# Two constant tiles multiplied by TensorE in the waits of three LayerNorms

## What is computed

```python
def _layer_norm(x):
    xc = x - jnp.mean(x, axis=-1, keepdims=True)
    return xc * lax.rsqrt(jnp.mean(xc * xc, axis=-1, keepdims=True) + LN_EPS)
...
        u = _layer_norm(h) * (1.0 + sc1) + sh1
        z = u @ w_in[l]
        ...
        mix = (gate_a * y_a + gate_b * y_b) @ w_out[l]
        h = _layer_norm(DEEPNORM_ALPHA * h + g1 * mix) * ln1_w[l] + ln1_b[l]
        u2 = _layer_norm(h) * (1.0 + sc2) + sh2
        a, bb = jnp.split(u2 @ w_ffn_in[l], 2, axis=-1)
        ffn = (jax.nn.silu(a) * bb) @ w_ffn_out[l]
        h = _layer_norm(DEEPNORM_ALPHA * h + g2 * ffn) * ln2_w[l] + ln2_b[l]
```

## Time and profile before

| | us |
|---|---|
| median of three runs | 3309.01 (3307.96 to 3311.09) |
| the profiled execution | 3308.02 |
| its span | 3305.9 |
| TensorE busy in it | 3128.1 (95%) |
| ScalarE, VectorE, GpSimd busy | 1085.3, 1153.4, 1440.2 |

### The profile page before, as it was taken

How to read it: one execution, slowest core, us unless ns; L and a number is a source line. 1 busy time by engine, 2 the same in 40 slices (tenths; PEclk the granted TensorE clock), 3 DMA queues, 4 the chain that set the end, 5 groups by cost and what they waited for, 6 DMA issues and landing times.

```text
span 3305.9 us, 52329 instructions
## 1 busy us (share of the span) xinstructions
PE 3128.1 (95%) x20668; PEld 2496.1 (76%) x20668; DVE 1153.4 (35%) x1637; ACT 1085.3 (33%) x1516; POOL 1440.2 (44%) x1824
## 2 busy tenths in 40 slices
PE   6998989988999899999988999999999999899999
PEld 4887768857887586887666888788688866688877
DVE  5016442332111355322555422225632255442210
ACT  2445453323222324112444322222411244432222
POOL 3542234634555363322415655566322241555555
PEclk7999889989999899999999999999999999999999
DMA  4223332212333232222414232233221241423233
GB/s 192 95 89 118 112 119 85 95 55 70 101 95 98 72 117 73 88 66 102 152 55 156 91 97 95 96 108 122 73 87 63 100 159 55 153 89 101 95 96 121
DMA packets 101407, 330.85 MB, mean 100 GB/s; under 512 B 9856, under 2 KB 10112, under 8 KB 100224
## 3 DMA queue, kind: packets, MB, share of 16 engines
q1 hardware_dynamic: 74656, 273.85, 25.3%
q10 hardware_dynamic: 26592, 54.66, 4.5%
HBM read 299.64 MB, written 28.84 MB: 99 GB/s over the span
## 4 chain that ended last, share of the span: by engine, by line
issue 41%; POOL 30%; PE 24%; DMA 1%; DVE 1%; ACT 1%; DVEq 0%; POOLq 0%; SPq 0%; ACTq 0%
POOL w_lo L310 30%; PE psum L339 19%; PE psum L620 4%; DMA w_raw<-in_fills 1%; DMA H<-scratch 1%; DVEq L1409 0%; PE psum L796 0%; POOLq L306 0%; PE psum L816 0%; PE psum L834 0%; POOLq L316 0%; DVE HL L1412 0%; PE psum L836 0%; DVE arena L1966 0%; PE psum L830 0%
## 5 line engine op out<-in xcount | busy, mean ns | idle before, releaser
L310 POOL TENSOR_TENSOR w_lo<-w_raw,w_hi 128x256 fp32r<-128x256 f32 x1820 | 1440.0, 822 | 1860.8 <-ACT w_hi L870 1664.9
L339 PE MATMUL psum<-XH,w_hi 128*128 128x512 f32 x2592 | 1061.8, 410 | 35.7 <-DVE XL L1412 22.5
L339 PE MATMUL psum<-XH,w_lo 128*128 128x512 f32 x2592 | 1021.2, 394 | 0.0
L339 PE MATMUL psum<-XL,w_hi 128*128 128x512 f32 x2592 | 1019.8, 393 | 0.0
L870 ACT ACTIVATE w_hi<-w_raw 128x1024 fp32r<-128x1024 f32 x436 | 460.2, 1056 | 813.6 <-PE psum L339 717.7
L339 PEld LDWEIGHTS psum<-XH,w_hi 128*128 128x128 f32 x2592 | 493.5, 190 | 174.0 <-issue 59.2
L339 PEld LDWEIGHTS psum<-XL,w_hi 128*128 128x128 f32 x2592 | 492.6, 190 | 106.3
L339 PEld LDWEIGHTS psum<-XH,w_lo 128*128 128x128 f32 x2592 | 493.7, 190 | 103.7 <-issue 9.4
L339 PE MATMUL psum<-HH,w_hi 128*128 128x512 f32 x976 | 391.6, 401 | 29.5 <-DVE HL L1412 21.5
L339 PE MATMUL psum<-HL,w_hi 128*128 128x512 f32 x976 | 387.0, 397 | 0.0
L339 PE MATMUL psum<-HH,w_lo 128*128 128x512 f32 x976 | 386.7, 396 | 0.0
(11 more groups left out here) (302 smaller groups left out, 2385.6 us busy)
## 6 DMA issues: line engine op xcount, KB each, us to landing
w_raw<-in_fills SPq DMA_DIRECT2D x488, 512.0 KB, 3.6
scratch<-arena ACTq DMA_DIRECT2D x86, 256.0 KB, 2.0
arena<-scratch ACTq DMA_DIRECT2D x10, 1024.0 KB, 8.7
arena<-in_w_ada SPq DMA_DIRECT2D x4, 2048.0 KB, 20.1
H<-scratch ACTq DMA_DIRECT2D x4, 2048.0 KB, 15.7
scratch<-H SPq DMA_DIRECT2D x2, 2048.0 KB, 8.5
arena<-scratch ACTq DMA_DIRECT2D x2, 2048.0 KB, 9.9
arena<-scratch ACTq DMA_DIRECT2D x2, 1792.0 KB, 20.8
```

The costliest lines, as they stand in the source:

```text
L310: ins = nc.gpsimd.tensor_tensor(w_lo[:, to:to + FILL // 4], w_raw[:, of:of + FILL // 4], w_hi[:, to:to + FILL // 4].bitcast(F32), ALU.subt ...
L339: ins = mm(out_ap, wt[:, w:w + 128], xt[:, x0:x0 + T], start=first and k == 0 and o == 0, stop=last and k == n - 1 and o == 2)
```

## The change

A new function idle_products(n) multiplies ones (128x128) with the constant chunk_start (128x512, zeros and ones) n times into bank 7. layer_norm calls it in front of its wait for acc (2), behind the products of the sum (2, but not in norm 0), and behind the products of the squares (6, in norm 3 10, in norm 0 none). Nothing reads what it writes. The function all_out of TensorE's part, which nothing called, goes.

```diff
             def layer_norm(n, src, sq, ready=None, acc=0):
 
                 if acc:
+                    idle_products(2)
                     pe.wait_ge(sem("acc"), acc)
                     ins = mm(bank(4), C("ones", 128), A(ACC_KB), start=True, stop=True)
                 else:
@@ -411,16 +412,20 @@
                             ready(t)
                         ins = mm(bank(4), C("ones", 128), src(t), start=t == 0, stop=t == DT - 1)
                 ins.then_inc(sem("ln_sum"), 1)
+                if n:
+                    idle_products(2)
                 for t in range(DT):
                     if t % 2 == 0:
                         pe.wait_ge(sem("ln_sq"), 4 * n + t // 2 + 1)
                     ins = mm(bank(5), C("ones", 128), sq(t), start=t == 0, stop=t == DT - 1)
                 ins.then_inc(sem("ln_var"), 1)
-
-            def all_out(c):
-
-                for b in range(4):
-                    pe.wait_ge(chunk_out[b], c)
+                if n:
+                    idle_products(10 if n == 3 else 6)
+
+            def idle_products(n):
+
+                for _ in range(n):
+                    mm(bank(7), C("ones", 128), C("chunk_start", T), start=True, stop=True)
```

## The result

The changed kernel takes 3287.93 us (median of 4, 3286.77 to 3290.02) against 3308.49 on the same chip (3307.26 to 3311.09). The ratio is 0.9938, with a 95% interval of 0.992 to 0.9955: a gain of 20.6 us. The forecast was 9.5 us, with a range down to 3296.0, so the direction was right and the size was not.

What follows compares the result with a forecast made beforehand. TensorE, busy for 95% of the span, was taken to bound the kernel. Stage gains of 10.62 us, less 1.0 for a further clock fall and 0.1 for the lead-ins, gave 9.5: 3299.5 us, range 3296 to 3304.5.

Steps and rivals of the forecast that it cites:

- The squares: Stages of squares in norms 2, 3 and 4: each falls to 7.13 us, winning 2.19, 1.58 and 2.68 us.
- The FFN gemm's start: First nine matmuls behind norm 3: 3.76 us at half clock become 2.04, winning 1.72 us.
- The one fall: One further clock fall in the LayerNorms despite the products: costs about 1.99 us, even chance, 1.0 us taken off.
- The full 10.62: Sum in us of all stage gains in norms 2 to 4 if the clock holds everywhere.
- The start of block two: First gemm behind norm 4: gain 0, because the rms product waits for VectorE's sum of squares anyway.
- the lead-ins: Two products in front of the sums of norms 2 and 4: 0 to 0.3 us delay each, 0.1 taken off.
- D: Rival, chance 0.06: clock is down while products run, they overrun their waits; 15.1 us slower, no gain, 3324.
- B: Rival, chance 0.11: short gaps don't matter, only the six and ten products hold the clock; gain 4.2 us, 3304.8.
- C: Rival, chance 0.06: products of one constant with another in an unread bank don't hold the clock; no change, 3309.0.
- What is won stays won: the gemms behind are TensorE's: Behind the LayerNorms: the gain lasts to the end, as later waits are relative to work that moves up too.
- The change adds to TensorE alone: ... no transfer is added: Whole kernel: 32 calls, 27.4 us at full clock, on TensorE; no other engine gets an instruction, no semaphore moves.
- a little for falls elsewhere that no longer come: Outside the LayerNorms: small extra gain beyond 10.62 us, setting the range's fast end at 3296.

Runs made afterwards that it cites:

- the one with loops: Changed kernel with its six and ten products in hardware loops, norm 4's six and one of its pair before the sum left out: 3296.4 us, -11.35 against the kernel before.
- the tails of 32 and 80: Kernel before with 32 or 80 one-column products at the very end of TensorE's program: -0.9 and +19.9 us, with 5.4 and 25.3 us of tail of their own.

## Why the prediction was right and wrong

**The LayerNorms, right.** Forecast 9.5 us, measured 8.9 in the traces of the changed kernel and of the one with loops. The whole time with the loops, where the number of fetches is as before, is 11.35 us less (6.6 to 14.9). Term by term:

- The squares came to the 7.13 us that the earlier trace rows gave, in all three norms. The FFN gemm's start won 1.66 of the 1.72 us.
- The one fall that the forecast gave an even chance did come, once, at the sum of norm 3. It cost 8.83 - 7.13 = 1.70 us where 1.99 was the price. The full 10.62 less that is 8.92, and the traces show 8.9. With eight products in place of six it is gone.
- The start of block two is worth nothing: the rms product stands 19.80 us behind the last square, as said.
- A product takes 0.86 us a call (12 records from 711.05 fill 5.16 of the 7.23 us wait), all groups fit, and the lead-ins delay nothing: norm 2's sum starts at 700.55, 0.24 ahead of the kernel before, which is where TensorE stood already.
- D's price of 15.1 us is put down to "all six groups"; the change has eight, and the sum prices the seven that would overrun.

**B is false**: the short waits matter most. With the long waits filled alone norm 4 has gaps of 1.8 and 2.4 us in front of its squares, and they ran at 0.70 in 10.07 us; with a pair of products in each gap they ran at 1.00 in 7.13. **C and D are false**: behind products of two constants all three stages of squares ran at 1.00, and no group overran.

**The step that failed** is "What is won stays won: the gemms behind are TensorE's", with "The change adds to TensorE alone: ... no transfer is added". It took the rest of the kernel as fixed. The change adds to one more thing, the length of TensorE's program, and with it the time of the weight loads changed. The runs show that crossing from 126 to 127 fetches of instructions is worth about 3 to 7 us by itself: 6.0 (7.3 without its own tail) with 22 products at the end, 3.3 between the two kernels with loops, 6.3 and 5.4 before the tails of 32 and 80, and 5.2 as the difference of the two groups of traces. The added instructions need not run anywhere near the work that gets faster.

A second term of the same step was too small: "a little for falls elsewhere that no longer come", which put the lower end at 3296, 2.4 us below what the full 10.62 gives. In block two alone the time that TensorE takes for the same matmuls goes from 2064.4 to 2078.4 us over the twenty traces, and the kernel before, on whose trace the forecast was built, is the one with 2078.4.

**Why some waits of TensorE were there to be shortened.** The earlier trace rows show TensorE busy 2078.80 of 2153.10 us, and the prediction read the other 74.30 as waits relative to TensorE's own work. They hold 7.8 us for the gates behind the reload of H, whose end a transfer sets; the idle time of the whole stretch is what fell by 3.0 us on average with 127 fetches. The waits for the conditioning matrices (17.3 us in the kernel before) lie ahead of the LayerNorms, between 245 and 455 us, where the prediction looked for no gain. They are 15.6 to 19.0 us in the traces with 126 fetches and 11.3 to 14.0 in those with 127, but for 16.2 with 32 products at the end.

**What stays open.** Three things. Why a longer program makes transfers faster: a different place of data or code in memory is the author's guess, and no run shows it; a scratch tensor of another size and a longer program of VectorE did not do it. Nor did any run find the length at which the step lies: 15 products in norm 0 have 126 fetches, 22 at the end have 127. Second, the sum does not close: 8.9 in the LayerNorms and 3 to 7 from the step leave 5 to 9 of the 20.6 us. A rival stands here that no run excludes, a gain in proportion to the products added ahead of block two: 8, 14, 15 and 32 narrow products in norm 0 gained 2.4, 4.4, 3.4 and 10.8 us, 0.2 to 0.3 each, the first three without the step. In their traces TensorE's busy time in block two is shorter by 10 to 14 us, and its idle time hardly changes or grows. One trace of each kernel can't tell whether the added products bring it about or whether these executions happened to have it. Third, the kernel with the long waits filled alone won 0.6 us in the LayerNorms and 17.5 in all, more outside than any other; 11.6 of the 12.0 us by which its block two is shorter are TensorE's busy time, so this is the same open question.

## What to carry to other kernels

Where TensorE waits a few microseconds for a relay of other engines, put cheap products of constants into an unread bank. Here they kept the granted clock at 1.00 in stages that had run at 0.72 to 0.82, and the short waits needed them more than the long ones: filled alone the short ones won 5.8 us in the LayerNorms, the long ones 0.6. Size each group to end just ahead of the release. Price the gain from a stage of the same work that the trace shows at full clock, and read it by stage: the whole time also moves by things such as the program's length, here 6 us for 22 products at the very end, and with the clock that one execution happens to get. So compare an edit of a few tenths of a per cent with a control of the same program length, and don't take waits on transfers as fixed.

## What the runs showed of the hardware

- 22 products of one column that run behind all other work of TensorE made the kernel 6.0 us (0.2%) faster, with the same 488 weight loads landing 3.2 instead of 3.6 us after their issue. With 15 in norm 0, or 128 more instructions on VectorE, the loads stayed at 3.7.
- With plain float32 products of ones with a tile of zeros and ones in front, the three stages of squares ran at a granted clock of 1.00 in 7.13 us each, the time that real data took in norm 0.
- At a granted clock of 1.00 the changed kernel's gemm matmuls of 128x512 start 0.227 us apart (eleven from 779.62 to 781.89) and have records of 0.39 us; at 0.50, in the kernel before, they start 0.427 us apart (eight from 753.30 to 756.29), nearly all with records of 0.63. Over the whole span the mean granted clock was 0.971 in the kernel before and 0.975 in the changed one.
- Whether the clock falls is not told by the gap in front alone. In the changed kernel TensorE idles for 2.07 us ahead of norm 3's sum, which runs at 0.81, and for 2.56 us (11.15 - 8.59) ahead of the FFN gemm, whose first nine matmuls run at 1.00. With the long waits filled alone the same gap in front of the FFN gemm (11.18 - 8.59 = 2.59 us) is followed by a mean of 0.62, where the first four matmuls start 0.24 to 0.30 us apart and the next ones 0.42:

```profile
739.27:750.45 11.18, 8.59 (x21) 3.48 (x20) 9.64 (x14) 5.28 (x7) 0.00 (x0) 1.00 0.00 0
750.45:753.50 3.05, 3.04 (x9) 2.42 (x10) 3.05 (x3) 1.22 (x1) 0.00 (x0) 0.62 0.00 0
```
